# A two-block network on one core: the first token mixer's order of work

## The chip, the cores and the metric

One Trainium2 chip, one of its cores. The metric is the device time of one execution in microseconds (us); runs of one kernel are compared by their median. An execution has a span (first to last instruction, read from the trace) and a little time around it.

## What is computed

The network takes 256 tokens of 1024 and 256 context tokens. Only the first block's mixer matters here (the experts behind it and the second block are unchanged):

```python
hx = modulate(rms_norm(x), shift, scale)          # shift, scale, gates: silu(c) @ w_ada, six vectors of 1024
hc = modulate(rms_norm(ctx), ...)
z  = h @ w_in + b_in                              # for hx and hc
q, k, v, o, gates, ga, gb = split(z)              # 256, 256, 512, 512, 16, 512, 512 columns
u  = ga * sigmoid(gb)                             # only for hx
# mLSTM in chunks of 128, 4 heads, forward and backward: log f = log_sigmoid(gate), b = cumsum(log f),
# r = log i - b, running maxima of r, states over the chunks of ctx, then of x, then outputs h
yx = concat([group_norm(h) * sigmoid(o),
             silu(layer_norm(depthwise_conv31(u) + conv_b))]) @ w_out + b_out
x  = x + gate * rms_norm(yx)
```

The ada products of the second block (adb0 to adb5) depend on c alone and are made in the same stage.

## The kernel before

One program, float32 throughout the mixer, an order written out by hand for each engine, with semaphores between them. Each engine runs its own list strictly in order.

- **Weights** come through three buffers of 4 MB (BUF 0 to 2), one item at a time in the order of ITEMS (line 70): ada0, ada1, in_qkv, ada2, in_og, ada3, in_conv, ada4, ada5, adb0 to adb5, w_out. Item i goes to buffer i mod 3 when TensorE has raised stream_used for item i-3 (SyncE, lines 415 to 454). Behind them, in the same SyncE queue, come the first expert weights (lines 466 to 489).
- **An ada item** (lines 873 to 903, ScalarE 669 to 682) is 16 matmuls into PS5 and PS6 (ada_parts), two copies by ScalarE (line 673), then the sums over the four row groups: 8 matmuls of 3 columns (line 898), or 2 of 512 for a gate (line 893), and ScalarE's copy. A matmul in float32 is two records in the trace.
- **The start.** TensorE turns all vectors (lines 866 to 871), VectorE copies them (1493 to 1495), ScalarE takes Silu of c (666), then ada0. Norms of x and ctx: ScalarE 684 to 691, VectorE 1505 to 1513. Turns 914 to 919, evicted with the modulation into hT (VectorE 1525) and hTc (ScalarE 702).
- **Projections** (TensorE 946 to 989): q, k, k of ctx, v of four chunks, ada2, o, gates, ada3, then the convolution's two halves in four groups. VectorE evicts each (1533 to 1569). They rotate over PS0 to PS4.
- **Gate chain**: log f (ScalarE 716 to 718, VectorE 1594), its cumulative sums on TensorE (991 to 994), eight row maxima: VectorE makes a diagonal (1610), TensorE spreads it (1001), VectorE masks and reduces (1622 to 1624). Then the scalar chain 1625 to 1654, ScalarE's Exp (721 to 726), k scaled (1644), six states (TensorE 1015, VectorE 1669 to 1673).
- **The depthwise convolution**: 31 taps on four channel groups, each tap one elementwise instruction of 128x256. GpSimd does group 3 and half of group 2 after all four inputs u are there (lines 607 to 614), VectorE groups 0 and 1 (conv_taps, 1570 to 1581) and the other half of group 2 (split_taps), spread between the links of the gate chain and of the output loop.
- **Output loop** over four (chunk, direction) pairs (TensorE 1042 to 1057, VectorE 1693 to 1717): an ada item's parts, output matmuls (1051, 1052), the item's sums, next rows.
- **Tail**: group norm (1722 to 1729), the convolution's layer norm by ones-matmuls (1064, 1075) with VectorE 1733 to 1744, then ScalarE's Silu (747), then w_out (TensorE 1079 to 1091): for each of four output banks first the mixer's half of the rows, after them the convolution's half. GpSimd loads the gate rows' biases after hn_ready (616 to 620), VectorE adds them (1752).

## Time and profile before

| | us |
|---|---|
| median of 3 runs | 1616.96 (1616.76 to 1621.95) |
| the profiled execution | 1620.79 |
| its span | 1619.0 |
| TensorE busy | 1290.5 (80%) |
| VectorE busy | 365.8 (23%) |
| ScalarE busy | 194.5 (12%) |
| GpSimd busy | 96.1 (6%) |

In the profile PE is TensorE's matmul, PEld its weight load, DVE VectorE, ACT ScalarE, POOL GpSimd, SP SyncE; PEq, SPq and so on are the engines' sequencers. L882 is line 882 of the kernel. A line of a timeline has the start, the duration, the engine, the line, the operation, what it writes and reads, and how many instructions were merged; in brackets the idle time before it and what ended it. PEclk is the granted TensorE clock as a share of 2.4 GHz, its other level being 1.2 GHz.

### The profile page before, as it was taken

The numbers are of one execution on the slowest core, as the hardware profiler recorded it, in microseconds if no ns is written. First come the engines' busy times: TensorE is split into PE (matmuls) and PEld (weight loads), VectorE is DVE, ScalarE is ACT, GpSimd is POOL, SyncE is SP. The second block draws the span as 40 slices with busy tenths as digits, with TensorE's granted clock in tenths as the row PEclk, the third lists the DMA queues.
The fourth block names the chain that finished last, engine by engine and source line by source line (L and its number), as shares of the span: only waits on it lengthen the run. The fifth ranks groups of instructions, "written<-read, shape, count | busy, mean of one in ns | idle before, by whom it ended". The sixth has DMA issues, their size and how long they took to land.

```text
span 1619.0 us, 20072 instructions
## 1 busy us (share of the span) xinstructions
PE 1290.5 (80%) x8173; PEld 669.0 (41%) x8173; DVE 365.8 (23%) x878; ACT 194.5 (12%) x372; POOL 96.1 (6%) x127
## 2 busy tenths in 40 slices
PE   4999679869999998999994998897656757656654
PEld 2747335435655655655652744443312212212211
DVE  1200789653111111111102133235100000000002
ACT  2100111121111111111112001102100000000001
POOL 1000892000000000000000000000000000000000
PEclk9999777879999999999998899998878777878877
DMA  9555568524899999999998442252799999999993
GB/s 375 189 200 215 211 262 351 196 104 159 311 374 420 421 421 420 420 421 421 412 420 314 176 165 93 112 207 107 315 421 421 421 422 422 422 422 422 422 422 162
DMA packets 84714, 509.59 MB, mean 315 GB/s; under 512 B 8480, under 2 KB 9848, under 8 KB 35096
## 3 DMA queue, kind: packets, MB, share of 16 engines
q1 hardware_dynamic: 82920, 502.97, 76.3%
q0 software_dynamic: 1520, 5.39, 0.9%
q8 instruction: 58, 0.95, 0.2%
q14 instruction: 24, 0.20, 0.0%
q10 hardware_dynamic: 192, 0.08, 0.0%
HBM read 507.36 MB, written 1.06 MB: 314 GB/s over the span
## 4 chain that ended last, share of the span: by engine, by line
PE 56%; DMA 30%; DVE 9%; SPq 2%; issue 2%; ACT 1%; DVEq 0%; ACTq 0%
DMA W<-in_w_expert_down 11%; DMA W<-in_w_expert_up 10%; PE PS L1321 9%; DMA W<-in_we_up 8%; PE PS L931 6%; PE PS L1188 4%; PE PS L1334 4%; PE PS L1390 3%; PE PS L1175 3%; PE PS L1468 3%; PE PS L1480 3%; PE PS L882 2%; PE PS L1350 2%; PE PS L1088 2%; PE PS L1448 2%; PE PS L1433 2%
## 5 line engine op out<-in xcount | busy, mean ns | idle before, releaser
L1468 PE MATMUL PS<-W,scr 128*32 128x512 f32 x1024 | 173.7, 842 | 131.0 <-DMA W<-in_w_expert_up 67.1
L1321 PE MATMUL PS<-W,scr 128*32 128x256 f32 (+2 forms) x2048 | 196.7, 402 | 23.0 <-DMA W<-in_we_up 21.9
L1912 DVE TENSOR_TENSOR scr<-scr,PS 128x256 f32<-128x256 f32 (+1 forms) x34 | 24.1, 708 | 670.1 <-PE PS L1468 387.1
L1321 PEld LDWEIGHTS PS<-W,scr 128*32 128x32 f32 (+2 forms) x2048 | 127.0, 133 | 100.8 <-issue 52.9
L1468 PEld LDWEIGHTS PS<-W,scr 128*32 128x32 f32 x1024 | 40.1, 147 | 263.5 <-issue 110.3
L1188 PE MATMUL PS<-scr 128*128 128x512 f32 x272 | 125.3, 603 | 2.6 <-ACT scr L787 2.6
L1480 PE MATMUL PS<-W,scr 128*32 128x512 f32 x512 | 70.2, 698 | 35.9 <-DMA W<-in_w_expert_down 34.9
L1175 PE MATMUL PS<-scr 128*128 128x128 bf16 x1632 | 96.7, 219 | 0.4 <-DVE scr L1896 0.4
L1334 PE MATMUL PS<-W,scr 128*32 128x512 f32 (+2 forms) x512 | 94.9, 597 | 0.7 <-DVE scr L1915 0.7
L1175 PEld LDWEIGHTS PS<-scr 128*128 128x128 bf16 x1632 | 93.9, 98 | 2.2 <-DVE scr L1867 1.2
L776 ACT COPY scr<-PS 128x512 f32<-128x512 f32 x68 | 39.9, 587 | 432.7 <-PE PS L1175 432.7
L1188 PEld LDWEIGHTS PS<-scr 128*128 128x128 f32 x272 | 49.2, 189 | 68.0 <-issue 67.8
L787 ACT COPY scr<-PS 128x512 f32<-128x512 f32 x68 | 36.5, 589 | 219.7 <-PE PS L1480 125.7
L1390 PE MATMUL PS<-W,hT 128*128 128x512 f32 x128 | 57.1, 599 | 0.0
L882 PE MATMUL PS<-W,sc 128*32 128x512 f32 x384 | 52.9, 700 | 4.2 <-ACT sc L666 2.7
L1480 PEld LDWEIGHTS PS<-W,scr 128*32 128x32 f32 x512 | 17.5, 125 | 82.2 <-DMA W<-in_w_expert_down 41.9
L1334 PEld LDWEIGHTS PS<-W,scr 128*32 128x32 f32 (+2 forms) x512 | 28.3, 126 | 47.0 <-issue 43.9
L931 PE MATMUL PS<-hT,W 128*128 128x256 f32 x192 | 45.1, 400 | 1.4 <-DVE hT L1525 1.4
L613 POOL TENSOR_SCALAR scr<-scr,convw 128x256 f32<-128x256 f32 x44 | 45.6, 1037 | 4.3
L931 PEld LDWEIGHTS PS<-hT,W 128*128 128x128 f32 x192 | 38.6, 202 | 7.6 <-DVE hT L1525 1.8
L781 ACT ACTIVATE scr<-PS 128x256 f32<-128x256 f32 (+1 forms) x34 | 14.8, 434 | 220.8 <-PE PS L1468 143.8
L1915 DVE COPY scr<-PS 128x256 f32<-128x256 f32 (+1 forms) x34 | 16.6, 488 | 100.3 <-PE PS L1206 100.3
(412 smaller groups left out, 1186.7 us busy)
## 6 DMA issues: line engine op xcount, KB each, us to landing
W<-in_we_gate SPq DMA_DIRECT2D x64, 1024.0 KB, 18.1
W<-in_we_up SPq DMA_DIRECT2D x64, 1024.0 KB, 16.2
W<-in_we_down SPq DMA_DIRECT2D x64, 1024.0 KB, 15.6
W<-in_w_expert_gate SPq DMA_DIRECT2D x64, 1024.0 KB, 18.8
W<-in_w_expert_up SPq DMA_DIRECT2D x64, 1024.0 KB, 19.0
W<-in_w_expert_down SPq DMA_DIRECT2D x64, 1024.0 KB, 19.4
W<-in_w_ada SPq DMA_DIRECT2D x12, 4096.0 KB, 14.1
W<-in_w_in SPq DMA_DIRECT2D x6, 4096.0 KB, 17.4
```

The costliest lines, as they stand in the source:

```text
L613: step(g.tensor_scalar(tmp, upad[:, i, :, j:j + ROW], convw[:, 4 * j + i:4 * j + i + 1], None, ALU.mult))
L776: a.copy(hTe[:, 4 * q:4 * q + 4, :], PS[4 + q][:].rearrange("p (k s) -> p k s", k=4)).then_inc(S["x_hTe"], 1)
L787: a.copy(Y[:, h * 512:(h + 1) * 512], PS[6 + h][:]).then_inc(S["x_Y"], 1)
L882: last = mm(PS[5 + h][32 * j:32 * j + 32, :], sc[:, 2 * j + kk, :], ada_w[n][:, 2 * j + kk, h * 512:(h + 1) * 512], start=(kk == 0), stop= ...
L931: last = mm(PS[t % 5][:, at:at + n], lhs(k), rhs(k), start=(k == 0), stop=(k == KD - 1))
L1175: last = mm(PS[4 + k // 4][:, (k % 4) * P:(k % 4 + 1) * P], hs[:, part, b, k * P:(k + 1) * P], Sb[:, b, :], start=(q == 0), stop=(q == NB ...
L1188: last = mm(PS[2 * b + h][:, :], Ct[:, b * P:(b + 1) * P], Y[:, h * 512:(h + 1) * 512], start=False, stop=False)
L1321: m = mm(PS[4 + kind][j * cap:(j + 1) * cap, 0:F1], hTe[:, k, j * cap:(j + 1) * cap], piece_view((g, kind, j))[:, k, :], start=(k == 0), s ...
L1334: m = mm(PS[6 + h][j * cap:(j + 1) * cap, :], aT[:, c, j * cap:(j + 1) * cap], piece_view((g, 2, j))[:, c, h * 512:(h + 1) * 512], start=( ...
L1390: last = mm(PS[6 + n % 2][:, :], hT[:, k, b * P:(b + 1) * P], w2k[2 + half][:, k, h * 512:(h + 1) * 512], start=(k == 0), stop=(k == KD - 1))
L1468: m = mm(PS[bank][j * CAP2:(j + 1) * CAP2, :], hTe[:, k, j * CAP2:(j + 1) * CAP2], gu2[piece][:, j, kk, :], start=(k == 0), stop=(k == KD ...
L1480: m = mm(PS[6 + h][j * CAP2:(j + 1) * CAP2, :], aT[:, c, j * CAP2:(j + 1) * CAP2], dn2[piece][:, j, cc, h * 512:(h + 1) * 512], start=(c = ...
```

## The change

- **Buffers and order of the weights.** STREAM gives for each item its buffer, USED the order in which TensorE uses them. in_conv is loaded third and in_og fourth; in_qkv keeps buffer 1 while ada2 to ada5, adb0 and adb1 go through the other two. The expert ring starts at slot 0, which is again the buffer freed first.
- **The start.** c, c_ctx and c_2 come by three loads of their own into cvec; the ada weights are laid out to match. TensorE does ada0 first, then the turns of the vectors and of x, then ada1. The norm and turns of ctx come later.
- **Projections.** The convolution's come first, then o and the gates, then q, k and v, mixed with ada2 to ada5, the cumulative sums and the eight row maxima. GpSimd begins with group 0 when u of group 0 is there, then half of group 1. VectorE's taps (groups 2 and 3, and half of 1) stand between its evictions; all are done before the states.
- **Buffers in SBUF**: diagonals in xn, accumulators of the convolution and gate parts in gate2 (free until adb2 and adb5).
- **Layer norm of the convolution** between the states and the loop, its Silu ahead of the loop's first Exp; the first output matmuls wait for it (PS7).
- **w_out**: the convolution's half of the rows first, into all four banks; the mixer's half after the turned heads.

The diff, cut to its core:

```diff
-SLOTS, SLOT_WORDS, RING0 = 12, 2048, 4
+SLOTS, SLOT_WORDS, RING0 = 12, 2048, 0
...
-ITEMS = ["ada0", "ada1", "in_qkv", "ada2", "in_og", "ada3", "in_conv", "ada4", "ada5",
-         "adb0", "adb1", "adb2", "adb3", "adb4", "adb5", "w_out"]
-AT = {n: i for i, n in enumerate(ITEMS)}
...
+STREAM = [("ada0", 0), ("ada1", 1), ("in_conv", 2), ("in_og", 0), ("in_qkv", 1), ("ada2", 2), ("ada3", 0), ("ada4", 2), ("ada5", 0),
+          ("adb0", 2), ("adb1", 0), ("adb2", 1), ("adb3", 2), ("adb4", 0), ("adb5", 1), ("w_out", 2)]
+USED = ["ada0", "ada1", "in_conv", "in_og", "ada2", "ada3", "ada4", "ada5", "in_qkv",
+        "adb0", "adb1", "adb2", "adb3", "adb4", "adb5", "w_out"]
+AT = {n: i for i, n in enumerate(USED)}
+HOME = dict(STREAM)
+TURN = {n: [b for _, b in STREAM[:i + 1]].count(s) for i, (n, s) in enumerate(STREAM)}
...
-        cacc = hT_words[:, 1024:2048].rearrange("p (c t) -> p c t", c=4)
+        diag = xn[:, 0, :].rearrange("p (b h t) -> p b h t", b=2, h=HEADS)
...
+        cacc = gate2[:, 1, :].rearrange("p (c t) -> p c t", c=4)
         hm = xn[:, 0, :].rearrange("p (b n) -> p b n", b=NB)
         qk = xn[:, 1, :].rearrange("p (c h t) -> p c h t", c=2, h=HEADS)
         usig = xn[:, 1, :].rearrange("p (c t) -> p c t", c=4)
...
+            for v, ap in enumerate((A["c"][0], A["c_ctx"], A["c_2"][0])):
+                sp.dma_start(cvec[:, v, :], ap.rearrange("(p k) -> p k", k=KD)).then_inc(S["c_loaded"], 16)
+            def stream(n):
...
+                p = [m for m, s in STREAM[:STREAM.index((n, HOME[n]))] if s == HOME[n]]
+                if p:
+                    sp.wait_ge(S["stream_used"], AT[p[-1]] + 1)
+                loaded = S[f"stream_loaded{HOME[n]}"]
...
+            stream("ada0")
+            sp.dma_start(x[:], A["x"][0].rearrange("(b p) d -> p b d", p=P)).then_inc(S["x_loaded"], 16)
...
+            sp.dma_start(vecs[0:TAPS * 4, 2, :], A["conv_w"][0].rearrange("t (c p) -> (t c) p", p=P)).then_inc(S["vec_loaded"], 16)
+            stream("ada1")
+            stream("in_conv")
+            sp.dma_start(ctxt, A["ctx"][0].rearrange("(b p) d -> p b d", p=P)).then_inc(S["ctx_loaded"], 16)
+            stream("in_og")
+            row(rowb, A["b_in"][0][256:1552])
...
-            pool.wait_ge(S["u_ready"], 4)
-            for i, taps in ((3, TAPS), (2, SPLIT_TAP)):
+            for i, taps in ((0, TAPS), (1, SPLIT_TAP)):
+                pool.wait_ge(S["u_ready"], i + 1)
                 acc = cacc[:, i, :].rearrange("p (r t) -> p r t", r=ROWS)
                 step(g.tensor_scalar(acc, upad[:, i, :, 0:ROW], convw[:, i:i + 1], cols[:, C_CONVB + i:C_CONVB + i + 1], ALU.mult, ALU.add))
...
-            vec(0, C_C, A["c"][0], 8)
-            vec(0, C_CTX, A["c_ctx"], 8)
-            vec(0, C_2, A["c_2"][0], 8)
...
             act.wait_ge(S["consts"], 1)
-            act.wait_ge(S["cols_ready"], 1)
+            act.wait_ge(S["c_loaded"], 48)
             for v in range(3):
-                step(a.activation(sc[:, :, v], cols[:, 8 * v:8 * v + 8], ACT.Silu), S["sc_ready"], wait=False)
...
+            first_norm(0, x, "x_loaded")
+            ada("ada0")
+            act.wait_ge(S["bias_mm"], 1)
+            step(a.copy(biasrow, PS[7][0:HEADS2, 0:T + P - 1]))
+            act.dma_start(bias_dram, biasrow).then_inc(S["bias_stored"], 16)
             ada("ada1")
...
             act.wait_ge(S["bias_stored"], 16)
+            act.wait_ge(S["cols_ready"], 1)
+            first_norm(1, ctxt, "ctx_loaded")
+            for i in range(4):
+                act.wait_ge(S["proj_mm"], 1 + i)
+                step(a.activation(usig[:, i, :], PS[i][:, T:2 * T], ACT.Sigmoid,
+                                  bias=cols[:, C_BCONV + 4 + i:C_BCONV + 5 + i]), S["usig_ready"], wait=False)
...
+            act.wait_ge(S["proj_ev"], 2)
+            step(a.activation(osig, osig, ACT.Sigmoid), S["osig_ready"], wait=False)
             ada("ada2")
-            ada("ada3")
...
+            act.wait_ge(S["norm_ms"], 3)
+            step(a.activation(crstd, crstd, ACT.Sqrt), S["norm_root"])
+            for i in range(4):
+                act.wait_ge(S["cn_ready"], 1)
+                step(a.activation(mixT[:, 4 + i, :], ctmp[:, i, :], ACT.Silu, scale=cols[:, C_LNG + i:C_LNG + i + 1],
+                                  bias=cols[:, C_LNB + i:C_LNB + i + 1]), S["mixT_conv"], wait=False)
             for gi, n in enumerate((None, "adb2", "adb3", "adb4", "adb5")):
...
+            ada_parts("ada0")
             pe.wait_ge(S["sel_ready"], 1)
-            ada("ada0")
...
+            ada_sums("ada0")
+            vectors_turned()
...
+            pe.wait_ge(S["cols_ready"], 1)
+            first_turns(0, xn)
+            ada("ada1")
...
+            pe.wait_ge(S["h_ready"], KD)
+            weights("in_conv")
+            for m in range(4):
+                project(m, [(0, T, feat(w_conv, m * P), alltoks(hT)), (T, T, feat(w_conv, 512 + m * P), alltoks(hT))])
+            pe.wait_ge(S["proj_mm"], 4)
+            pe.sem_inc(S["stream_used"], 1)
+            pe.wait_ge(S["ada_ready"], ada_done[2])
+            first_turns(1, ctxt)
+            weights("in_og")
+            for b in range(NB):
+                pe.wait_ge(S["u_ready"], b + 1)
+                project(b, [(0, 512, toks(hT, b), wcols(w_og, 0, 512))])
...
+            pe.wait_ge(S["u_ready"], 3)
...
+            pe.wait_ge(S["proj_mm"], 7)
+            pe.sem_inc(S["stream_used"], 1)
+            ada_parts("ada2")
+            pe.wait_ge(S["proj_ev"], 3)
+            pe.wait_ge(S["u_ready"], 4)
...
+            ada_sums("ada2")
+            weights("in_qkv")
+            project(0, [(m * T, T, feat(w_qkv, m * P), alltoks(hT)) for m in range(2)])
...
+            project(1, [(m * T, T, feat(w_qkv, 256 + m * P), alltoks(hT)) for m in range(2)])
...
+            largest(0)
+            largest(1)
+            project(2, [(m * T, T, toks(hTc, m), wcols(w_qkv, 256, 256)) for m in range(2)])
+            largest(2)
+            largest(3)
+            pe.wait_ge(S["proj_ev"], 6)
...
+            ada("ada3")
...
+                project(bank, [(0, 512, toks(src, b), wcols(w_qkv, 512, 512))])
...
+            values(0, 2, 1, 6)
+            largest(4)
+            largest(5)
+            values(1, 3, 2, 7)
+            largest(6)
+            largest(7)
+            ada("ada4")
+            values(2, 0, 0, 8)
             ada("ada5")
+            values(3, 1, 1, 9)
+            pe.wait_ge(S["proj_mm"], 16)
+            pe.sem_inc(S["stream_used"], 1)
...
+                    pe.wait_ge(S["proj_ev"], 12)
...
+                    pe.wait_ge(S["conv_ready"], 1)
+                    pe.wait_ge(S["conv_taps"], 2 * TAPS + 1)
+                    for i in range(4):
+                        last = mm(PS[2][:, 0:T], ones[:], cacc[:, i, :], start=(i == 0), stop=(i == 3))
+                    last.then_inc(S["cmean_mm"], 1)
+                if j < 2:
+                    ada(("adb0", "adb1")[j])
...
+            pe.wait_ge(S["csq_ready"], 1)
+            for i in range(4):
+                last = mm(PS[7][:, 0:T], ones[:], cacc[:, i, :], start=(i == 0), stop=(i == 3))
+            last.then_inc(S["cvar_mm"], 1)
...
                     pe.wait_ge(S["hm_ready"], gi)
+                else:
+                    pe.wait_ge(S["cn_ready"], 1)
...
+            def mixed_out(part):
+                for b in range(NB):
+                    for h in range(2):
+                        for k in range(4 * part, 4 * part + 4):
+                            last = mm(PS[2 * b + h][:, :], mixT[:, k, b * P:(b + 1) * P], w_o[:, k, h * 512:(h + 1) * 512],
+                                      start=(k == 4), stop=(k == 3))
+                        if not part:
+                            last.then_inc(S["stream_used"] if b and h else S["proj_mm"], 1)
             pe.wait_ge(S["hm_ready"], 4)
-            pe.wait_ge(S["conv_ready"], 1)
-            pe.wait_ge(S["conv_taps"], 2 * TAPS + 1)
-            for i in range(4):
-                last = mm(PS[4][:, 0:T], ones[:], cacc[:, i, :], start=(i == 0), stop=(i == 3))
-            last.then_inc(S["cmean_mm"], 1)
+            pe.wait_ge(S["mixT_conv"], 4)
+            weights("w_out")
+            mixed_out(1)
...
             pe.wait_ge(S["mixT_m"], 2)
...
+            mixed_out(0)
...
+            conv_input(0)
+            conv_input(1)
+            split_taps(SPLIT_TAP, 23)
+            conv_input(2)
+            split_taps(23, TAPS)
+            conv_input(3)
+            dve.wait_ge(S["row_loaded"], 176)
...
+            conv_taps(0, 5)
+            for b in range(NB):
+                dve.wait_ge(S["proj_mm"], 5 + b)
+                step(v.tensor_tensor(osig[:, b, :], PS[b][:], rowb[:, 768:1280], ALU.add), ev)
+                if b == 0:
+                    conv_taps(5, 9)
...
+            conv_taps(9, 12)
...
+            dve.wait_ge(S["osig_ready"], 1)
+            step(v.tensor_tensor(osig, osig, outer(normg, 2), ALU.mult))
+            conv_taps(12, 14)
             dve.wait_ge(S["exp_out"], 1)
             step(v.scalar_tensor_tensor(out=LF, in0=lf, scalar=0.0, in1=lft, op0=ALU.min, op1=ALU.subtract), S["lf_ready"])
...
+            conv_taps(14, 17)
+            dve.wait_ge(S["proj_mm"], 9)
...
+            def diagonal(into, col, buf, sem):
+                step(v.tensor_tensor(into[:, buf, :, :], outer(ident[:], 4), inner(col, P), ALU.mult), sem, wait=False)
+            def largest(g):
                 dve.wait_ge(S["row_mm"], g + 1)
-                bank = PS[1 + g % 2][:].rearrange("p (h s) -> p h s", h=4)
+                if g < 6:
+                    diagonal(diag, r_[:, 4 * g + 8:4 * g + 12], g % 2, S["diag_ready"])
+                bank = PS[3 + g % 2][:].rearrange("p (h s) -> p h s", h=4)
...
+            for g in range(2):
+                diagonal(diag, r_[:, 4 * g:4 * g + 4], g, S["diag_ready"])
+            conv_taps(17, 20)
+            dve.wait_ge(S["proj_mm"], 10)
...
+            largest(0)
+            largest(1)
+            dve.wait_ge(S["proj_mm"], 11)
...
+            largest(2)
+            largest(3)
+            dve.wait_ge(S["proj_mm"], 12)
...
+            conv_taps(20, 24)
+            values(0, 2, 1)
+            largest(4)
+            largest(5)
+            conv_taps(24, 26)
+            values(1, 3, 2)
+            largest(6)
+            largest(7)
             step(v.tensor_tensor(wst, r_, rmax, ALU.subtract), S["exp_in"])
@@ -1636,14 +1710,6 @@
                     step(v.tensor_tensor(e_log[:, q], rmax[:, at:at + 4], mx_[:, q], ALU.subtract))
                     step(v.tensor_tensor(m_run[:, 8 * j + 8 + 4 * d:8 * j + 12 + 4 * d], bt_[:, at:at + 4], mx_[:, q], ALU.add))
                 step(v.tensor_tensor(a_log, m, mx_, ALU.subtract), S["exp_in"] if j == 2 else None)
...
-            conv_taps(8, 10)
+            conv_taps(26, 28)
+            dve.wait_ge(S["exp_out"], 2)
+            dve.wait_ge(S["proj_mm"], 14)
...
+            values(2, 0, 0)
+            conv_taps(28, TAPS)
+            dve.wait_ge(S["conv_ready"], 2)
+            step(v.tensor_tensor(cacc[:, 1, :], cacc[:, 1, :], cacc2, ALU.add), S["conv_taps"])
+            values(3, 1, 1)
...
+            for gi in range(2):
+                diagonal(diagm, m_t[:, 4 * gi:4 * gi + 4], gi, S["diagm_ready"])
+            states(0)
+            dve.wait_ge(S["cmean_mm"], 1)
+            step(v.tensor_scalar(cmean, PS[2][:, 0:T], 1.0 / CONV_C, None, ALU.mult))
+            step(v.tensor_tensor(ctmp, cacc, outer(cmean, 4), ALU.subtract))
+            step(v.tensor_tensor(cacc, ctmp, ctmp, ALU.mult), S["csq_ready"])
+            states(1)
+            states(2)
+            dve.wait_ge(S["cvar_mm"], 1)
```

## Rows read from the trace of the kernel before

**Rows 1.** the page, part 4: shares of the chain that ended last

```profile
PE 56%; DMA 30%; DVE 9%; SPq 2%; issue 2%; ACT 1%; DVEq 0%; ACTq 0%
```

**Rows 2.** window table: start:end, length, engines busy (instructions), clock, DMA, GB/s

```profile
49.00:164.00 115.00, 109.27 (x452) 71.45 (x453) 11.67 (x25) 6.93 (x14) 0.00 (x0) 0.97 0.48 186
164.00:196.00 32.00, 21.61 (x69) 9.88 (x69) 24.86 (x39) 6.78 (x10) 28.30 (x31) 0.68 0.67 263
196.00:240.40 44.40, 30.86 (x205) 15.74 (x204) 35.74 (x81) 6.43 (x15) 40.19 (x47) 0.77 0.58 218
240.40:289.20 48.80, 47.86 (x234) 24.51 (x233) 41.33 (x105) 8.25 (x16) 12.10 (x14) 0.79 0.84 332
```

**Rows 3.** chain of waits, 0 to 50 us: start, us, what

```profile
23.54 6.19 PE PS L882 x32
...
37.05 4.53 PE PS L882 x32
...
45.70 3.72 DVE hT L1525 x8
```

**Rows 4.** DMA issues of 0 to 10 us: KB, us to landing; ada0, x, ada1

```profile
W<-in_w_ada SPq DMA_DIRECT2D x1, 4096.0 KB, 13.3
x<-in_x SPq DMA_DIRECT2D x1, 1024.0 KB, 15.7
...
W<-in_w_ada SPq DMA_DIRECT2D x1, 4096.0 KB, 23.2
```

**Rows 5.** chain of waits, 70 to 265 us

```profile
72.37 27.48 PE PS L931 x64
100.14 3.67 PE PS L882 x32
103.84 1.08 ACT ada_rows L673 x2
...
134.25 29.43 PE PS L931 x128
...
236.69 1.95 PE PS L898 x16
...
260.95 3.90 PE PS L898 x16
```

**Rows 6.** timeline, ScalarE's two exponentials of the scalar chain

```profile
198.38 0.23 ACT L723 ACTIVATE scr<-scr 128x32 f32<-128x32 f32 x1 [23.44 <-DVE scr L1625]
204.88 0.24 ACT L723 ACTIVATE small<-small 128x48 f32<-128x48 f32 x1 [6.27 <-DVE small L1638]
```

**Rows 7.** timeline, VectorE's taps beside GpSimd and alone

```profile
171.15 5.41 DVE L1580 SCALAR_TENSOR_TENSOR hT<-scr,convw,hT 128x256 f32<-128x256 f32 x8
...
268.63 3.25 DVE L1580 SCALAR_TENSOR_TENSOR hT<-scr,convw,hT 128x256 f32<-128x256 f32 x8
```

**Rows 8.** line 613: ns min/median/max of the multiplies, first and last start

```profile
L613 POOL TENSOR_SCALAR scr<-scr,convw x44: 924/973/1987, 165.6 to 251.9; 128x256 f32<-128x256 f32 x44
```

**Rows 9.** chain of waits, 289 to 336 us

```profile
292.79 0.70 DVE xn L1717
...
298.37 1.24 DVE xn L1729
...
306.40 28.59 PE PS L1088 x64
```

**Rows 10.** timeline of the tail: root's reciprocal, Silu, the gate rows

```profile
307.48 1.75 DVE L1743 RECIPROCAL scr<-scr 128x256 f32<-128x256 f32 x1 [0.61 <-ACT scr L744]
...
310.57 1.28 ACT L747 ACT_TABLE_LOAD   x1 [3.19 <-DVE scr L1744]
...
311.86 2.08 ACT L747 ACTIVATE scr<-scr,cols 128x256 f32<-128x256 f32 x4
...
312.33 3.74 DVE L1752 TENSOR_TENSOR gate<-gate,scr 128x1024 f32<-128x1024 f32 x3 [1.84 <-DMA hT<-in_b_ada]
```

**Rows 11.** SyncE's queue, 330 to 420 us: waited for, us, times, longest

```profile
SPq L482 <- PE PS L1279: 40.7, 1, 40.7
```


## What I expect

> **What bounds the kernel now.** I read the page first: the chain that ended last runs through TensorE for 56% of the span and through DMA for 30% [rows 1]. That is a mean over unlike stages, so I read the window table by stage next. The change touches only the first mixer, from the start to about 335 us. There TensorE is nearly full from 49 to 164 us (109.3 of 115 us, granted clock 0.97), then thins out: 21.6 of 32 us at clock 0.68, 30.9 of 44.4 us at 0.77, and 47.9 of 48.8 us at 0.79 [rows 2]. The clock has two levels, 1.2 and 2.4 GHz; a mean of 0.68 is a stretch at 1.2 GHz for two thirds of its time. VectorE, by contrast, is busy for 11.7 of the 115 us of the projections and for 35.7 of 44.4 us after them. So in the first mixer nothing but TensorE's own order sets the end until 164 us, and after that VectorE's serial gate chain, with the convolution's taps between its links, sets it while TensorE waits in short pieces and mostly at its lower level. Such a stage gains by putting the two kinds of work side by side.
>
> **Does a gain in the mixer last to the end?** After w_out, SyncE's next expert loads wait for TensorE: its queue sat 40.7 us on the matmul of line 1279, the shared expert's [rows 11]. All loads behind that one are released by TensorE's use of earlier ones and by the sorting of the experts, which follow the mixer. So both the TensorE part and the DMA part behind it move by what the mixer gains, one for one. The sum can be made at one event: the last matmul of w_out, 335.0 us.
>
> **Part 1, the start.** Before, ada0 started at 23.54 us [rows 3], behind the landing of all vectors, their turns, the copies of the results and Silu. Now c comes by three loads of its own ahead of ada0. Its weights landed 13.3 us after issue at 0.8 us, x 15.7 us after 1.27 us [rows 4]; three more issues ahead cost about 1.2 us, so ada0 starts near 15.4 and x is in at 18.2. But the gain doesn't last. ScalarE squares x (2.5 us) and takes the root with a table load before it copies ada0's parts, so the copies end near 23.7; 16 sums (2.6), the turns of the vectors and the bias matmul (2.2) and the 16 turns of x (3.6) follow one another at 1.2 GHz on TensorE, and ada1 starts near 32.2 instead of 37.05 [rows 3]. Its weights would be in at 30.1 (28.9 now [rows 4], plus 1.2) and do not hold it. in_conv, now third in the queue, lands about 10.5 us later still, near 41, before h is ready. **-4.7 us** at h ready (49.4, then 44.7). The norm and turns of ctx are moved behind; ScalarE and VectorE do them beside in_conv's matmuls, and only TensorE's 16 turns stay on the path.
>
> **Part 2, from h ready to the loop over the four head groups** (49.4 to 240.4, 191 us). In the new order I count TensorE's work at 2.4 GHz and add the waits by name. One 512-wide matmul record costs 27.48/64 = 0.429 us, a 256-wide one half of it, 0.215 (the 128 in a row cost 0.230 with their slow start) [rows 5].
> - Projections: 224 records of 256 and 96 of 512: 48.1 + 41.2 = 89.3.
> - Parts of six ada items at 3.67 [rows 5]: 22.0. Four sums at 1.95 [rows 5] and two gate sums at four 512-records: 11.2.
> - Copy wait between parts and sums, 1.1 each [rows 5], five times (ada2's is covered by the gate parts): 5.5.
> - Eight row maxima of two 512-records and four for the m rows: 8.6. Turns of ctx, gate projection, gate sums, states, q times k: 2.7 + 2.6 + 1.6 + 3.4 + 3.0 = 13.3, estimates from their records with the slow ones halved.
> - The convolution's two sums of 8 256-records, moved here from the tail: 3.4.
>
> These make 153. Waits: start of in_conv at the lower clock 2; ada4's sums, since ScalarE must do the exponentials of two chain results before it copies ada4. Now the first result was used at 198.4 and the second at 204.9 [rows 6]; that 6.5 us becomes about 4.5 without taps of GpSimd in between, of which 3 is not under ada4's parts; small gaps between groups 5. That is 163. The cover for VectorE's chain is the q, k and v projections; where it fails the wait stands in full. Last, the clock. A few ada waits and turns in a row will drop it. Before, 76 us from 164 to 240 ran at 0.68 to 0.77; I take three drops of 2 us, the size of a sum at 3.90 against 1.95 [rows 5]: +6. Bounds: none, and 24 if every sum and short matmul of the list (11.2 + 13.3) takes twice its time. 169 against 191: **-22 us**.
>
> **The weights.** in_qkv now holds one of three buffers until about 182, so adb0 to adb5 and w_out stream through late. adb2 is asked for at 182, lands near 195 and is wanted at 208; adb5 is asked for when adb2 is used (212), lands near 226, wanted near 250; w_out after it, near 240, wanted at 265. With 13.3 us per item [rows 4] none holds TensorE. Nothing else waits behind these on SyncE.
>
> **Part 3, the loop.** Twelve taps of VectorE per group leave it, but TensorE was busy 47.9 of its 48.8 us [rows 2], so that frees nothing. One wait is new: the first output matmuls wait for the normalised convolution, and ScalarE puts four Silu with a table load ahead of the group's first Exp. From cvar: root with table load 1.7, reciprocal 1.75, product 1.24, Silu with a table load before and after 1.28 + 2.08 + 1.28 [rows 10], of which the first load hides; this ends near 7.7 us after loop start, where now it is 4.2. Behind it wait TensorE's matmuls and all of the loop. **+3.5 us** (bounds 1 and 6).
>
> **Part 4, the tail.** Now, from the last output matmul at 289.2: heads done 293.5, group norm and gate 299.6, variance and the turned heads to 306.4, w_out 28.6, end 335.0 [rows 9]: 45.8 us. New: 4.3 to heads done, convolution half 13.7 + 1.5 slow start while VectorE does the norm (6.1, fully hidden), eight turns 1.9, copy 0.9, mixer half 13.7: 36.0. **-9.8 us**. What is late next is not the gate rows: their loads, issued after the norm, let VectorE start at 312.3, 12.7 us after it, and six adds and products at 1.25 (3.74/3) with three short ones follow, 8.3 us [rows 10]; together 21 us, and w_out's last matmul comes 25 us after the norm. The first products of the output wait, the last does not.
>
> **Sum:** -4.7 - 22 + 3.5 - 9.8 = **-33.0 us**. The profiled execution took 1620.8, so 1587.8; it lies 3.8 above the median of the runs shown (1616.96), and by that median the forecast is **1584.0**.
>
> **A rule against the change.** 48 to 64 of VectorE's taps now stand beside GpSimd's and ahead of evictions. The trace: eight taps took 5.41 us beside GpSimd and 3.25 alone [rows 7], 0.68 against 0.41. GpSimd's chain ran 86.3 us from its first to its last multiply [rows 8], with ends 88.7; it should now run from 55 to 144, and is wanted at 172. The Trainium skill, "SBUF — State Buffer", section on who interferes with whom, says that with two SBUF inputs the later of the two engines is blocked for the whole instruction of the other. By that every tap could wait out a GpSimd instruction; the rows show a third of that on average.
>
> **Rivals.**
> - *VectorE becomes the bound* (0.16). If each of about 64 taps takes GpSimd's multiply time, 0.97 us [rows 8], instead of 0.68, VectorE is 19 us later by 145 us; its slack ahead of the gate results, the k and first v evictions takes up about a third. Cost 14: -19, 1598.0. For: its fill of those stretches goes from 10% to about 80%. Against: the eight-tap row.
> - *The clock holds and the waits are hidden* (0.15). TensorE is fed without a wait over 2 us; the 6 us of clock go, part 3 costs 1 instead of 3.5: -41.5, 1575.5. Against: even beside the projections a 2 us wait shows before.
> - *The clock falls for good* (0.04), the slower side. Between 95 and 208 us there are some 104 us of TensorE work, cut by copies and short matmuls. At a mean clock g they cost 104(1/g - 1) more, less the 6 counted. At 0.68, the clock of 164 to 196 [rows 2]: 43, a net +10, 1627. It decides below 0.73. Against: those stretches had TensorE busy 68%, these would have it over 90%, like the stretch at 0.97. The Trainium skill, "TensorE: Matmul & The Clock Gate", part 4, says that turns by matmul don't raise the clock; the 16 turns of ctx now stand between two projections. By that the next 2 us would run at half, +1 us.
> - *The stages behind absorb it* (0.03): the expert loads would then not follow the sorting; about 1617. [rows 11] speaks against.
>
> **How the numbers follow.** Forecast 0.62, its own range 1576 to 1600 (clock 0 to 24 in place of 6 and part 3 1 to 6 in place of 3.5, taken together as -8 and +16). The range reaches down past the second rival and up past the first: **1573 to 1601**, leaving out the third and fourth and the edges, about 0.15 in all. About 0.3%, 4.9 us, can be told from no change. Faster by more: 0.93; within: 0.03; slower: 0.04.
>
> **What would show it.** In the changed profile: ada0 near 15 us and in_conv's first matmul near 45; GpSimd's first tap near 55 and its last near 144; TensorE over 90% busy from 45 to 180 with a clock over 0.95, and over 0.85 to 208; the loop's first m matmul near 210; a wait of some 4 us before the first output matmul; w_out in two halves, last matmul near 302 (335.0 - 33). Wrong, if VectorE's evictions of q, k or v hold TensorE for more than 3 us in one place, if an ada item's weights end a wait, or if the end of w_out and the end of the kernel move by different amounts.

## The result, and the profile after the change

| | before | after |
|---|---|---|
| median of the runs | 1617.76 us (4 runs) | **1590.01 us** (4 runs, 1587.35 to 1590.49) |
| ratio to before | | 0.982, 95% interval 0.9803 to 0.9836 |
| profiled execution | 1620.8 us, span 1619.0 | 1590.05 us, span 1588.2 |
| last matmul of w_out ends | 335.0 us | 306.8 us |

The change is faster by 27.8 us (1.7%); 33 us were forecast, and the range of 1573 to 1601 holds the time. The medians moved by 27.8 us, w_out's end by 28.2 us in the profiles. The spans differ by 2.6 us more, because the profiled execution of before took 1284.0 us from w_out's end to its own end, the one of after 1281.4. I therefore go by w_out's end.

The windows of the changed kernel, in the same columns as those of before [rows 2]: the start, the projections while GpSimd has taps, the rest of k and v, the group up to the loop, the loop, the tail.

```profile
core 0: us, PE busy (x) PEld busy (x) DVE busy (x) ACT busy (x) POOL busy (x), PEclk, DMA share, GB/s
4.00:45.10 41.10, 21.22 (x117) 11.63 (x117) 7.63 (x23) 9.69 (x20) 2.69 (x11) 0.82 1.02 399
45.10:134.80 89.70, 87.18 (x414) 62.87 (x415) 64.06 (x111) 15.15 (x27) 69.79 (x79) 0.96 0.59 225
134.80:171.00 36.20, 32.98 (x96) 15.60 (x97) 18.02 (x60) 3.32 (x8) 9.23 (x12) 0.79 0.50 196
171.00:216.67 45.67, 41.09 (x242) 22.17 (x241) 15.13 (x30) 7.43 (x14) 0.00 (x0) 0.93 0.80 305
216.67:271.00 54.33, 49.08 (x234) 26.03 (x234) 20.86 (x61) 12.89 (x22) 0.00 (x0) 0.78 0.76 298
271.00:307.00 36.00, 32.44 (x76) 14.06 (x76) 20.59 (x34) 3.71 (x6) 3.93 (x7) 0.95 0.53 193
```

VectorE and GpSimd now work beside the projections: 64 and 70 us in the second window, where VectorE had 11.7 in 115 us before. TensorE stays 97% busy there. Two windows stand out against the forecast: 134.8 to 171 at a clock of 0.79, and the loop, 54.3 us long instead of 48.8, again at 0.78.

The waits of TensorE from h ready to the loop, and in the loop (line and what it waited for: total, times, longest, in us):

```profile
PE PS L918 <- ACT ada_rows L685: 6.9, 4, 3.2
PE PS L913 <- ACT ada_rows L685: 1.9, 2, 1.2
PE PS L1059 <- DVE scr L1688: 0.9, 1, 0.9
...
PE PS L1106 <- DVE scr L1791: 4.9, 1, 4.9
```

No eviction of q, k or v is among them, and no weights of an ada item. The largest is the new one of the loop. The chain of work that ended last (start us, us, what) shows what surrounds the slow places, first in the projections:

```profile
131.01 3.96 PE PS L918 x16
134.97 9.48 PE PS L952 x16
...
146.17 6.87 PE PS L952 x16
...
160.41 1.08 ACT ada_rows L685 x2
...
161.54 3.96 PE PS L918 x16
...
197.48 1.95 PE PS L918 x16
```

then around the start of the loop:

```profile
216.02 1.76 DVE scr L1768
...
217.81 1.24 DVE scr L1769
...
219.11 1.28 ACT L752
...
220.41 1.47 ACT scr L752 x3
...
222.50 1.28 ACT L758
...
224.46 0.70 DVE scr L1791
...
225.20 0.80 PE PS L1106 x2
226.00 0.72 PE PS L1107 x2
```

and in the tail:

```profile
275.23 15.70 PE PS L1120 x32
...
292.81 14.02 PE PS L1120 x32
```

What is called a v half here is the v projection of one chunk, 16 records of 512. It takes 6.87 us at one place and 9.48 at another, directly behind a group of sums (L918) that takes 3.96 us. From 154.8 to 160.1 us, left out in this view, the chain is VectorE's, small instructions one after another behind the last row maximum; ScalarE's exponential and ada4's copy follow, and they end the longest wait of the list, 3.2 us. The loop's first output matmul waits for the reciprocal (1.76), the product (1.24), a table load (L752, 1.28), four Silu, the next table load (L758, 1.28) and the exponential's product. Then its pairs of records take 0.72 us each; in the next group a pair takes 0.42. w_out's two halves stand as planned.

### The profile page after: what moved, and what is told of

It reads as the page before. It is cut to its first block, busy times and chain, and to the rows that moved or that the text cites. A ratio compares the mean times of both kernels' runs of the same rounds, so it can differ in the third digit from the quotient of the medians.

```text
span 1588.2 us, 20071 instructions
## 1 busy us (share of the span) xinstructions
PE 1285.0 (81%) x8173; PEld 665.6 (42%) x8173; DVE 362.1 (23%) x878; ACT 194.8 (12%) x372; POOL 94.8 (6%) x128
## 4 chain that ended last, share of the span: by engine, by line
PE 59%; DMA 30%; DVE 5%; SPq 2%; ACT 2%; issue 1%; DVEq 0%; ACTq 0%
DMA W<-in_w_expert_down 12%; DMA W<-in_w_expert_up 10%; PE PS L1367 9%; DMA W<-in_we_up 8%; PE PS L952 6%; PE PS L1234 5%; PE PS L1380 4%; PE PS L1436 4%; PE PS L1221 3%; PE PS L1514 3%; PE PS L1526 3%; PE PS L902 2%; PE PS L1120 2%; PE PS L1396 2%; PE PS L1494 2%; PE PS L1479 2%
## 5 line engine op out<-in xcount | busy, mean ns | idle before, releaser
L1514 PE MATMUL PS<-W,scr 128*32 128x512 f32 x1024 | 176.3, 853 | 128.5 <-DMA W<-in_w_expert_up 65.7
L1526 PE MATMUL PS<-W,scr 128*32 128x512 f32 x512 | 72.3, 716 | 32.8 <-DMA W<-in_w_expert_down 31.8
L902 PE MATMUL PS<-W,sc 128*32 128x512 f32 x384 | 50.4, 671 | 16.4 <-DMA W<-in_w_ada 15.7
L1380 PEld LDWEIGHTS PS<-W,scr 128*32 128x32 f32 (+2 forms) x512 | 28.3, 126 | 47.0 <-issue 43.9
## 6 DMA issues: line engine op xcount, KB each, us to landing
W<-in_w_expert_up SPq DMA_DIRECT2D x64, 1024.0 KB, 19.3
W<-in_w_expert_down SPq DMA_DIRECT2D x64, 1024.0 KB, 19.4
W<-in_w_ada SPq DMA_DIRECT2D x12, 4096.0 KB, 15.4
```

The costliest lines, as they stand in the source:

```text
L902: last = mm(PS[5 + h][32 * j:32 * j + 32, :], sc[:, 2 * j + kk, :], ada_w[n][:, 2 * j + kk, h * 512:(h + 1) * 512], start=(kk == 0), stop= ...
L1380: m = mm(PS[6 + h][j * cap:(j + 1) * cap, :], aT[:, c, j * cap:(j + 1) * cap], piece_view((g, 2, j))[:, c, h * 512:(h + 1) * 512], start=( ...
L1514: m = mm(PS[bank][j * CAP2:(j + 1) * CAP2, :], hTe[:, k, j * CAP2:(j + 1) * CAP2], gu2[piece][:, j, kk, :], start=(k == 0), stop=(k == KD ...
L1526: m = mm(PS[6 + h][j * CAP2:(j + 1) * CAP2, :], aT[:, c, j * CAP2:(j + 1) * CAP2], dn2[piece][:, j, cc, h * 512:(h + 1) * 512], start=(c = ...
```

## The experiments

All kernels compute everything. Medians are given. The variants ran in three groups, each beside the kernel before on one chip (1616.3, 1616.8 and 1616.8 us there). Differences between variants are differences of medians; the changed kernel itself ran in the first group only, so a difference across groups is uncertain by at least the 0.5 us between these three. The changed kernel as it is:

> The changed kernel itself, beside the others. Every theory: about 27.8 to 30.7 us under the kernel before (1590), end of w_out near 306.8 us.

1588.29 us (1587.65 to 1589.98), ratio 0.9824 (0.9805 to 0.9843). This is the reference for the other variants.

**The loop's start.** Two edits; first, only the Silu is moved behind the last exponential:

```
-            for i in range(4):
-                act.wait_ge(S["cn_ready"], 1)
-                step(a.activation(mixT[:, 4 + i, :], ctmp[:, i, :], ACT.Silu, scale=cols[:, C_LNG + i:C_LNG + i + 1],
-                                  bias=cols[:, C_LNB + i:C_LNB + i + 1]), S["mixT_conv"], wait=False)
             for gi, n in enumerate((None, "adb2", "adb3", "adb4", "adb5")):
...
                     step(a.activation(dts[gi % 2], dts[gi % 2], ACT.Exp, scale=-1.0), S["exp_out"])
+                if gi == 3:
+                    for i in range(4):
...
```

> The changed kernel with ScalarE's four Silu moved behind the loop's last Exp, and nothing else. They and one table load stand between cn_ready (219.1) and the first Exp (223.8): the first output matmul comes 3.4 to 4.6 us earlier, kernel 3 to 5 us less. If it brings nothing, VectorE's part of that chain was the bound.

1583.4 us (1582.49 to 1585.5), -4.9. The wait before the first output matmul went from 4.9 to 2.8 us, and the first five of the eight pairs of records took 0.42 to 0.49 us, the other three still 0.72. Second, the reciprocal and the product are put behind VectorE's first scores too, and TensorE waits for the variance only (`norm_ms`) before it reuses the bank:

```
-                    pe.wait_ge(S["cn_ready"], 1)
+                    pe.wait_ge(S["norm_ms"], 3)
...
-            dve.wait_ge(S["norm_root"], 3)
-            step(v.reciprocal(crstd, crstd))
-            step(v.tensor_tensor(ctmp, ctmp, outer(crstd, 4), ALU.mult), S["cn_ready"])
...
                 step(v.tensor_tensor(dts[gi % 2], dts[gi % 2], qk[:, c, :, :], ALU.mult), S["sT_ready"])
+                if gi == 0:
+                    dve.wait_ge(S["norm_root"], 3)
+                    step(v.reciprocal(crstd, crstd))
+                    step(v.tensor_tensor(ctmp, ctmp, outer(crstd, 4), ALU.mult), S["cn_ready"])
```

> The changed kernel, but ScalarE does the convolution's four Silu after the loop's last Exp, VectorE does the reciprocal and the product of the convolution's norm after the first group's scores, and TensorE's first output matmul waits only for PS7 to be read. Theory: the wait before the first output matmul (4.9 us, 8.5 us from loop start to it) is this chain and nothing else; it falls to under 1 us, and the matmuls behind it keep the higher clock more often (16 records of 0.42 instead of 0.73 us, gate sums 2.0 instead of 3.7): 4 to 11 us less, 1579 to 1586. Rival: the wait only moves, to the scores of the next groups or to the Silu ahead of w_out: within 1.5 us of the changed kernel.

1576.86 us (1575.7 to 1578.14), -11.4, just beyond the 4 to 11 us of its theory. The chain at the same place, in that kernel:

```profile
212.31 1.72 PE PS L1088 x4
214.02 3.57 PE PS L903 x32
217.60 0.42 PE PS L1107 x2
218.01 0.42 PE PS L1108 x2
...
220.94 1.93 PE PS L914 x4
```

The wait is gone, and with it the slow stretch: output records at 0.42, gate sums (L914) at 1.93 instead of 3.71. In the reference the first output matmul starts at 223.7 us and w_out ends at 305.3, here at 217.6 and 293.9: 6.1 us come ahead of that matmul, 4.9 of them the wait, and 5.3 behind it, 4.2 of them in the eight pairs of output records (8 x 0.3) and the gate sums (1.8) at the full clock.

**The sums behind the v projections.** For ada3, ada4 and ada5 a v projection stands between the parts and the sums, so that ScalarE's copy lies under it:

```
-            ada("ada3")
+            ada_parts("ada3")
             values(0, 2, 1, 6)
+            ada_sums("ada3")
...
-            ada("ada4")
+            ada_parts("ada4")
             values(2, 0, 0, 8)
-            ada("ada5")
+            ada_sums("ada4")
+            ada_parts("ada5")
             values(3, 1, 1, 9)
+            ada_sums("ada5")
```

> The changed kernel, but of ada3, ada4 and ada5 TensorE does the parts, then a v projection, then the sums, so that ScalarE's copies (and for ada4 the exponentials before them) run beside matmuls. Theory 'waits': the clock falls at 131 and 161 us because of the idle time of 1.25 and 3.22 us before the 16 narrow matmuls. Then 5.7 us of waits go, and with them the slow sums (2 x 2.0) and slow v halves (9.5 and 9.6 us instead of 6.9): 15 us less than the changed kernel, 1575. Rival 'narrow matmuls': 16 matmuls of 3 columns let the clock fall whether TensorE waited or not. Then only the 5.7 us go, 1584, and two sums at 3.96 us remain in the trace.

1581.2 us (1576.77 to 1585.31), -7.1. The median is nearer to 'narrow matmuls' (1584) than to 'waits' (1575), but its runs spread too far to decide by the time. The chain decides, and it fits neither reading:

```profile
128.04 7.06 PE PS L952 x16
135.11 3.57 PE PS L918 x16
138.68 3.28 PE PS L1015 x4
...
161.17 3.58 PE PS L918 x16
```

Here TensorE had no wait and was at full clock, and still the sums took 3.57 us, not 1.95. Only the row maximum behind them is slow, 3.28 us against 1.72 for the next one. Its windows (columns as above) say the same: full clock through the sums, the lower one only behind them:

```profile
136.00:137.00 1.00, 1.00 (x6) 1.00 (x5) 0.00 (x0) 0.00 (x0) 0.92 (x1) 1.00 1.07 426
137.00:138.00 1.00, 1.00 (x6) 1.00 (x5) 0.00 (x0) 0.00 (x0) 0.82 (x3) 1.00 0.99 406
138.00:139.00 1.00, 1.00 (x4) 1.00 (x5) 0.00 (x0) 0.27 (x2) 0.92 (x2) 0.53 1.02 422
```

So the clock is not why those sums are long. (ada4's sums, 161.17 to 164.7 us, had 1.00 throughout.) Both edits together:

> sums_later and loop_first together. If they are independent their gains add: 15 + 7, near 1568 by 'waits', near 1577 by 'narrow matmuls'. If the weights' stream (adb2 is asked for only after the last v projection) becomes the bound, the gains don't add and a wait for an ada load stands in the loop.

1569.04 us (1568.72 to 1571.58), -19.3; the single gains add to 18.5, the same within the spread of the runs. They are independent.

**Why some sums take 3.9 us.** The weight loads of the sums tell it. First ada3's in the kernel before, then adb0's in the same kernel (the form counts, durations in ns as min/median/max):

```profile
L898 PEld LDWEIGHTS PS<-small,ada_rows x16: 313/335/336, 130.3 to 133.8; 128*128 128x128 f32 x16
```

```profile
L898 PEld LDWEIGHTS PS<-small,ada_rows x16: 186/192/192, 236.7 to 238.4; 128*128 128x128 f32 x16
```

In both stretches the granted clock was 1.00, and the sums took 3.90 and 1.95 us. The shapes are equal, but for ada3, ada4, adb3 and adb4 the kernel takes `every_kd(ada_rows[:])[:, j, :]` as weights, every eighth column, and for ada0, ada1, adb0 and adb1 128 adjacent ones. The edit lets ScalarE's copy write the eights sorted, so that the sums read adjacent columns in both cases:

```
                 for h in range(2):
-                    step(a.copy(ada_rows[:, h * 512:(h + 1) * 512], PS[5 + h][:]), S["ada_rows_ready"], wait=False)
+                    if s in (3, 4):
+                        dst = ada_rows[:].rearrange("p (j i) -> p j i", j=KD)[:, :, 64 * h:64 * h + 64]
+                        step(a.copy(dst, every_kd(PS[5 + h][:])), S["ada_rows_ready"], wait=False)
+                    else:
+                        step(a.copy(ada_rows[:, h * 512:(h + 1) * 512], PS[5 + h][:]), S["ada_rows_ready"], wait=False)
...
-                        part = every_kd(ada_rows[:])[:, j, :] if ffn else ada_rows[:, j * P:(j + 1) * P]
+                        part = ada_rows[:, j * P:(j + 1) * P]
```

> The changed kernel; only for the four items ada3, ada4, adb3 and adb4 ScalarE's copies write the parts in the order in which the sums read them, so each of their 16 weight loads reads 128 adjacent columns instead of every eighth. Everything is computed. Theory 'stride': those sums take 3.9 us instead of 1.95 because a weight load of every eighth column takes 0.334 us against 0.192, at either clock; so each item saves 2.0, four 7.9, and with the clock no longer falling behind ada3's and ada4's sums the two v projections take 6.9 instead of 9.5: 1588.3 - 13 = 1575, or 1580.5 if the clock still falls. The copies now read PSUM with a stride; if that doubled their 0.54, 4.3 us would come back. Rival 'clock', my prediction's reading: the sums take 3.9 because TensorE is at 1.2 GHz there, and the layout changes nothing: 1588 (within 2).

1578.44 us (1575.66 to 1582.74), ratio 0.9769 (0.9756 to 0.9783), -9.9, between the 1575 and the 1580.5 of 'stride'. The rival 'clock' forecast no difference and falls. (The trace is of an execution of 1575.7 us.) The chain:

```profile
129.63 1.95 PE PS L921 x16
131.58 6.97 PE PS L955 x16
...
155.64 1.95 PE PS L921 x16
157.59 8.67 PE PS L955 x16
```

ada3's sums take 1.95 us, and the v half behind them 6.97 instead of 9.48: no lower clock there any more. Behind ada4's sums, which still follow a wait of 3.2 us, it is 8.67 instead of 9.57, at a mean clock of 0.81. In the loop adb3's and adb4's sums take 1.88 and 1.89 us instead of 3.90 and 3.91. The copies cost nothing more, 0.588 us each with the stride in their PSUM operand against 0.589:

```profile
L688 ACT COPY ada_rows<-PS 128x512 f32<-128x512 f32 x8 | 4.3, 588 | 28.7 <-PE PS L906 28.6
L690 ACT COPY ada_rows<-PS 128x512 f32<-128x512 f32 x16 | 8.6, 589 | 48.5 <-PE PS L906 48.4
```

> The same edit on the kernel that has the sums behind the v projections and the convolution's end behind the first scores (1569.0 in the first comparison). Everything is computed. 'Stride': ada3's and ada4's sums 3.57 to 1.8, adb3's and adb4's 3.9 to 1.95: -7.4, and the 3.5 us that the maxima and ada5's parts lose to the clock behind them go too: 1558 to 1562. 'Clock': 1569, since the sums are as long in either layout.

**1560.31 us** (1558.74 to 1563.01), ratio 0.9647 (0.9633 to 0.966), 8.7 below the 1569.0 without it: 3.5% under the kernel before and the fastest version, as 'stride' forecast (1558 to 1562). ada3's and ada4's sums take 1.68 and 1.69 us. adb3's and adb4's took 2.94 and 2.40 in its trace, not the 1.95 expected: their loads were adjacent ones, but the granted clock was 0.60 and 0.75.

**The tail.** w_out's mixer half first, as in the kernel before, both halves behind the turned heads:

```
-            pe.wait_ge(S["mixT_conv"], 4)
-            weights("w_out")
-            mixed_out(1)
...
             pe.wait_ge(S["mixT_m"], 2)
+            pe.wait_ge(S["mixT_conv"], 4)
+            weights("w_out")
             mixed_out(0)
+            mixed_out(1)
```

> The changed kernel with the old order of w_out: the mixer's half of the rows first, both halves after the turned heads. Theory: the convolution's half hides the group norm (6.1 us), its turns and copies partly; TensorE then idles from the last head to hn_ready and runs turns at the lower clock. 4.3 + 6.1 + 1.9 + 0.9 + 28.6 = 41.8 us from the last output matmul to w_out's end instead of 35.9: 6 us more than the changed kernel, and the other 4 of the tail's 10 us belong to the layer norm's earlier place. Rival: all of the 10 us are the order of the halves: 10 us more.

1595.24 us (1594.1 to 1596.22), +7.0, near the 6 of its theory and not the 10 of the rival. Its w_out is one piece that starts late:

```profile
276.54 1.95 PE PS L1131 x8
279.26 30.82 PE PS L1120 x64
```

**The start.** The turns of the vectors again ahead of ada0:

```
+            vectors_turned()
             ada_parts("ada0")
             pe.wait_ge(S["sel_ready"], 1)
             ada_sums("ada0")
-            vectors_turned()
```

> The changed kernel, but TensorE turns the vectors before ada0, so that ada0 waits for the landing of conv_w as before. Theory: ada0 starts 5 to 6 us later, 2.2 us of turns are out of the way, ScalarE's root at 22.4 us hides some: h ready 3 to 4 us later, whole kernel 3 to 4 us slower than the changed one. Rival: the start is hidden by the norm of x and the loads: no difference.

1589.65 us (1587.94 to 1590.94), +1.4, which the intervals don't tell from nothing. Its trace has in_conv's first matmul at 47.9 us, 2.8 later than in the profile of after and 4.5 later than in that of the reference, whose starts differ by 1.6 themselves (ada0's sums took 3.54 us in the one, at clock 0.50, and 1.92 in the other); ada0 starts at 22.2 us behind this landing and the turns:

```profile
7.02 12.84 DMA scr<-in_conv_w
```

So ada0 and h are about as late as forecast, but the 3 to 4 us at the end of the kernel did not come. Of the delay 1.6 us are regained at once, in in_conv's 128 records (29.31 us, 30.88 in after). At the first output matmul, 225.3 us, nothing is left against after (225.2), and 1.6 against the reference (223.7); w_out ends at 306.6, in those two at 306.8 and 305.3. What the earlier ada0 is worth at the end is not told from nothing by these runs.

**VectorE's room.** VectorE takes 30 of the 31 taps of the second group instead of 16, GpSimd the first one only:

```
-            for i, taps in ((0, TAPS), (1, SPLIT_TAP)):
+            for i, taps in ((0, TAPS), (1, 1)):
...
-            split_taps(SPLIT_TAP, 23)
+            split_taps(1, 16)
             conv_input(2)
-            split_taps(23, TAPS)
+            split_taps(16, TAPS)
```

> The changed kernel, but VectorE does taps 1 to 30 of channel group 1 and GpSimd only tap 0: 15 more taps on VectorE (8 to 10 us of its time between 57 and 90 us), 15 fewer on GpSimd, which ends near 115. Theory: VectorE has room (it waits 30 us for v projections later, and its evictions catch up), TensorE doesn't notice: within 2 us of the changed kernel, u_ready 3 and 4 later by up to 8 us at most on a place where TensorE doesn't wait for them. Rival 'VectorE is the bound of 60 to 125 us': 5 to 9 us slower.

1588.19 us (1585.86 to 1588.77), -0.1. Fourteen more taps on VectorE (its expectation counted 15) cost nothing that the runs can tell.

## Why the prediction was right or wrong, point by point

At w_out's end 28.2 us came of the 33.0. The parts, forecast and measured:

| part | forecast | measured | from |
|---|---|---|---|
| 1, start | -4.7 | -4.4 | h ready 49.46, now 45.10 |
| 2, to the loop | -22 | -19.4 | 190.9, now 171.6 |
| 3, loop | +3.5 | +5.5 | 48.8, now 54.3 |
| 4, tail | -9.8 | -10.0 | 45.8, now 35.8 |

**Part 1** held at h ready: ada0's parts started at 15.7 (15.4), ada1's at 33.2 (32.2). But `vectors_first`, which gave 2.8 to 4.5 us of it up again, came out only 1.4 us slower, so how much of this part lasts to the end is not shown.

**Part 2**: the sum was nearly right, but one step of it was wrong. I took 1.95 us for each of the four sums, and for the clock three drops of the size 3.90 - 1.95, which is the difference of the two rows in [rows 5]. That difference is no clock: it is the stride of the weights. Under the sums of 3.90 us the granted clock was 0.91, and under ada3's in the same kernel, as long, it was 1.00. `contiguous` took the stride away and the sums fell to 1.95 where they stood. So ada3's and ada4's sums cost 4.0 us that I had not counted (2 x (3.96 - 1.95)). The lower clock cost, besides, 5.3 us in two v halves (9.48 and 9.57 against 6.87), 1.8 in the variance's sums (L1081: 3.72 in after, 1.92 in the kernel with both edits) and 3.4 at in_conv's start (30.88 against 27.48; 2 were counted). These are 14.5 us, where 8 stood in the sum. The rest, work and waits, came 3.9 us cheaper than the 161 in it: ada4's copy is the longest wait with 3.2 us, and no wait for q, k or v exists. That this made up for more than half of the 6.5 us counted too few is luck. I should have seen the stride: the two groups differ at the same line by 0.334 and 0.192 us in their weight loads, in a view that shows loads on a row of their own, and the code of the line has the two cases.

**Part 3**: the mechanism was right, its size too small. The wait was forecast as 3.5 us more (7.7 against 4.2); the first output matmul came 8.5 us after the loop's start, 4.3 more. What the sum left out was the clock behind the wait: all eight pairs of the first group's output records took 0.72 us or more, in the kernel before only two. From the first of them to the gate sums it is 5.9 us, before it was 4.0. That is 1.9 us more; other work of the loop came about 0.7 cheaper. The gate sums took 3.71 us in both, so they are no part of the growth. Of the kernel before:

```profile
247.19 0.73 PE PS L1051 x2
247.92 0.72 PE PS L1052 x2
248.64 3.71 PE PS L893 x4
```

Taking the wait away gave 11.4 us, more than the +5.5 by which the loop grew, in part because the kernel before paid some of it too: 1.8 us at these gate sums and 0.6 at two pairs. The rest of the difference isn't split up.

**Part 4** held: convolution half 15.7 us under VectorE's norm (forecast 15.2), mixer half 14.0. Undoing the order of the halves costs 7.0 us; from the first output matmul to w_out's end it has 89.1 us, the reference 81.6. I put the remaining 3 us down to the convolution's sums, which the change took out of the tail; that was not tested alone.

**Rivals.** *VectorE becomes the bound*: no. Its 46 taps beside GpSimd kept it busy for 28.3 us, 0.62 each (row below; the 0.68 forecast was 5.41 over eight; the 682 ns of the row is a mean of durations that overlap). No tap or eviction held TensorE in the projections: the 3.2 us wait for ada4's copy is the end of VectorE's scalar chain, which starts 0.1 us behind the last row maximum, so no tap delays it. Fourteen more taps changed nothing.

```profile
L1595 DVE SCALAR_TENSOR_TENSOR gate<-scr,convw,gate 128x256 f32<-128x256 f32 x46 | 28.3, 682 | 0.1
```

*The clock holds and the waits are hidden*: not in this kernel, but it is what the variants reach: 1569 with the waits hidden, 1560 with the stride gone, below the 1575.5 of this rival. *The clock falls for good*: no; the granted clock over 95 to 208 us is 0.92, far from 0.73. Nor did the 16 turns of ctx (1.94 us) lower it, or cost the 1 us named there: the 32 records behind them took 13.74 us, 0.429 each, at a clock of 1.00. *The stages behind absorb it*: no. From w_out's end to the end of the span the eleven profiles of kernels with the change have 1280.3 to 1283.7 us, and the one of before 1284.0, though w_out ends anywhere from 277.7 to 335.0. What is won in the mixer is won at the end, to within these 4 us. The prediction had called itself wrong if the two ends moved by different amounts; the 2.6 us between them in the profiles are within that spread.

**What would show it**: GpSimd's first tap came at 57.9 us (55), and its last ended near 145 (144). TensorE over 90% busy to 180 came true, a clock over 0.95 to 180 did not (0.91 in the mean, 0.79 from 134.8). The loop started at 216.7 instead of 210, and the last matmul of w_out ended at 306.8 instead of 302.

## What to carry to other kernels

When one line's groups of equal shape differ in time, look at its weight loads and its access pattern before putting it down to the clock; the window table decides, since it shows the granted clock under the very instructions. Count for each new wait of TensorE also the matmuls behind it at the lower clock: here 4.9 us without work were less than half of the 11.4 that went with them. Work that another engine needs only later (a normalisation, a table function) goes behind the links of the chain that TensorE waits for, and a copy between two matmul groups goes under a third group.

## What the runs showed of the hardware that I had not expected

A weight load of 128x128 float32 from adjacent columns took 0.192 us at full clock and 0.333 at the lower one; from every eighth column it took 0.335 at either. That it equals the price of the lower clock hid it. The rows of ada0's sums in after (adjacent, clock 0.50 from 23.9 to 27.4 us), of ada3's (strided, its window below at 1.00, then 0.51) and of ada4's (strided, its window at 0.50 throughout):

```profile
L918 PEld LDWEIGHTS PS<-small,ada_rows x16: 287/333/333, 23.9 to 27.0; 128*128 128x128 f32 x16
```

```profile
L918 PEld LDWEIGHTS PS<-small,ada_rows x16: 312/334/336, 131.0 to 134.6; 128*128 128x128 f32 x16
```

```profile
L918 PEld LDWEIGHTS PS<-small,ada_rows x16: 312/335/336, 161.5 to 165.1; 128*128 128x128 f32 x16
```

```profile
131.00:133.00 2.00, 1.99 (x9) 1.99 (x9) 2.00 (x4) 0.00 (x0) 1.82 (x3) 1.00 0.89 272
133.00:135.00 2.00, 2.00 (x10) 2.00 (x10) 2.00 (x4) 0.00 (x0) 1.82 (x3) 0.51 1.02 410
...
161.50:165.50 4.00, 3.96 (x17) 3.96 (x17) 3.93 (x13) 0.00 (x0) 0.00 (x0) 0.50 1.02 396
```

ScalarE reads PSUM with the same step of eight at no extra cost (0.588 against 0.589 us). The clock fell behind 16 strided sums even where TensorE had no wait (`sums_later`, 0.53 from 138 us), and did not fall behind 16 adjacent ones with a copy wait of 1.1 us ahead (`contiguous`, 6.97 us for the v half). But adjacent loads do not keep it up everywhere: in `both_contiguous` the parts of ada5 stand behind ada4's adjacent sums (1.69 us at clock 1.00) and a wait of 0.3 us, and take 5.34 us instead of 3.57, at about 0.68. What makes the clock fall behind the sums therefore stays open; only why the strided sums themselves are long is shown.
